# Attention stage reordered, last stage in four steps over blocks, zero fill in parts: one change to a two-layer decoder step on eight cores

## The chip, the cores and the metric

The kernel runs on one Trainium2 chip, as one program on all 8 of its cores, each with its own prompt of 2048 tokens and 16 of the 128 sample tokens. The metric is the device time of the slowest core in microseconds. An engine is TensorE (PE), VectorE (DVE), ScalarE (ACT), GpSimd (POOL) or SyncE (SP); each works through its own instructions in order and waits on semaphores.

## The reference, cut to what matters

```python
def run(x, p, conv_past, kv_past):                      # D = 1024
    h = x
    for i in range(2):
        hn = rms_norm(h, norm_mix[i])
        if i == 0:
            y = conv_module(hn, ...)                    # GLU, depthwise conv, layer norm, product
        else:
            q = project_q(hn, w_q, q_norm)              # 16 heads of 64, each head normed
            y = window_attention(q, k_sh, v_sh, sinks) @ w_o    # window of 128 keys, 4 key heads
        h = h + y
        hn = rms_norm(h, norm_ffn[i])
        h = h + (swiglu(hn) if i == 0 else moe_swiglu(hn))      # D_FF 2816; 8 experts, top 2, 3584 each
        h = h + sigmoid(rms_norm(h, norm_ple[i]) @ w_gate) * (p[i] @ w_proj)
        if i == 0:
            k_sh, v_sh = shared_kv(h)                   # keys normed
    return h, states
```

The outputs are both streams h, the last 30 rows of the convolution's input, and the last 128 keys and values of each sequence.

## The kernel before, in words

The work of a core is cut into blocks of 128 tokens: 16 prompt blocks and block 16 with the 16 sample tokens (NB = 17). The stages follow one another: convolution (to about 230 us), its second product and norms (to 380), the dense SwiGLU's gate and up products (to 727, lines L1353 to L1373, for each of 22 tiles f of the hidden width, over five column groups), its down product with the first per-layer embedding (to about 990), attention (to about 1610), the experts (to about 2858) and the last stage.

A small scheduler (`Sched`) writes waits from declared reads and writes. Every engine and DMA queue runs in the order in which the Python text emits instructions; this order is written by hand. A write has to wait for all earlier readers of its resource; with `part=True` it does not wait for other part writes. A tile `Res` marked `excl` (a PSUM bank) is handed over whole.

*Zeros.* `zerofill` (L325) writes zeros over the 5120 rows of XG, into which tokens are scattered for the experts, and over the 128 dummy rows of YD. Both are issued from ScalarE ahead of the loop over f, from tile `zt` (L1428). Ahead of them SyncE issues three copies of caches to the outputs (ks, vs, convs).

*Attention.* A loop of 21 turns (from L1939) works on several blocks at a time. In turn i block ord5[i] (the sample block is first) is turned for TensorE (`x3_turn`), gives keys and values (`kv_mm`) and queries (`q_mm` twice), is normed by head (`qk_norm` L1682, with the power on GpSimd at L1689), scaled (`qk_scale`) and turned (`qk_turn`, one turn later); block ord5[i-2] has its four groups of scores, exponentials, masks (L1762, L1764) and value products (`pv`, L1783) and is divided (`onorm` L1791 to L1795); the block before is multiplied by w_o (`oproj` L1814, L1819) and its sum normed (`o_norm`: square L944, epsilon on VectorE L948, power on GpSimd L949, scaling L1833); and the one before that is routed (`route_l` L343). `x3_scale` (square, epsilon, power, scaling L1639) prepares block i+1. All but scores and value products use three PSUM banks in rotation (`mb`). For groups of blocks (0 to 4, 5 to 9, 10 to 13, 14 and 15, and 16), `wave_a` and `wave_b` work out expert, rank and slot of each token on VectorE, and GpSimd scatters the normed rows (L161). In the middle of `wave_b` VectorE overwrites the slots that the scatters read (L432), and waits for them. For turns 2 to 5 the 16 sample tokens are attended over their caches at the end of the turn.

*Last stage.* `final_prep` loads the weights of the second embedding into ring slots that are free early, `final` allots the rest. Each block is in three steps: `st0` loads h (SyncE), p (GpSimd's queue), gathers its two expert outputs and turns p by a DMA transpose; `st1` adds the two outputs, weighted by the gates (L786, VectorE, twice), norms (`rstd` L337 to L340), scales (L792) and turns x by a DMA transpose; `st2` has the products (L812, L805), the sigmoid (L819), the gating product (L820) and the sum with h on GpSimd (L822). The second gather of a pair waits for the first one's landing (`part=(k == 1)`).

The central lines of the last stage's loop are these.

```python
for i in range(NB + 1):
    if i < NB:
        b[i] = st1(*a.pop(i))
    if i >= 1:
        st2(*b.pop(i - 1))
    if i + 3 < NB:
        a[i + 3] = st0(i + 3)
```

## Time and profile before

| | us |
|---|---|
| median of 3 runs | 3117.32 (3114.04 to 3370.99) |
| the profiled execution | 3120.35 |
| its span on the slowest core (3) | 3119.0 |
| spans of the eight cores | 3095.4 to 3119.0 |
| TensorE busy | 2466.9 (79%) |
| VectorE, ScalarE, GpSimd busy | 964.4, 743.6, 594.3 |

The profile is of one execution, on the slowest core. Times in it run from the span's start. An arrow `<-` in brackets names what ended the idle time before an instruction; SPq, ACTq and POOLq are the DMA issues of an engine. "x8" is a count of instructions. PEclk is the TensorE clock that was granted, as a share of 2.4 GHz: at any time it is one of 1.2 and 2.4 GHz, and a stretch shows the mean.

### The profile page before, as it was taken

How to read it: one execution, taken by the hardware profiler on the slowest of the kernel's cores; microseconds unless marked ns; L12 is line 12 of the kernel's file. 1: busy time of each engine (PE TensorE's matmuls, PEld its weight loads, DVE VectorE, ACT ScalarE, POOL GpSimd, SP SyncE). 2: the span in 40 equal slices, each digit the busy share in tenths (PEclk: the TensorE clock that was granted, in tenths of full speed). 3: DMA queues.
4: the chain of work that ended last, by engine and by line, in shares of the span. 5: the costliest groups of instructions: out<-in, count | busy, mean ns of one | idle time of the engine just before them, and what ended most of it. 6: DMA issues, size and time to landing. Idle time of an engine off the chain costs nothing.

```text
span 3119.0 us, 43753 instructions; the slowest of 8 cores (3095.4 to 3119.0 us)
## 1 busy us (share of the span) xinstructions
PE 2466.9 (79%) x18903; PEld 1687.7 (54%) x18911; DVE 964.4 (31%) x1492; ACT 743.6 (24%) x1074; POOL 594.3 (19%) x794
## 2 busy tenths in 40 slices
PE   5876749997998266656519999999999999996354
PEld 3453425553443033323218888887799888885111
DVE  4665502221333144444422121211122212120444
ACT  4215401111221354434302111111122111110111
POOL 1105400000000142232331111111121111110444
PEclk8988879998999578778759999999999999998677
DMA  7555584323222510110159999998899999962453
GB/s 194 105 110 139 144 205 72 58 38 65 72 72 72 170 48 30 41 64 31 58 122 177 170 183 167 184 168 154 136 171 181 173 178 177 175 103 66 127 145 94
DMA packets 156458, 377.44 MB, mean 121 GB/s; under 512 B 52424, under 2 KB 61768, under 8 KB 155264
## 3 DMA queue, kind: packets, MB, share of 16 engines
q0 software_dynamic: 69360, 230.65, 43.9%
q1 hardware_dynamic: 81616, 133.15, 14.7%
q10 hardware_dynamic: 5280, 10.75, 1.0%
q8 instruction: 151, 2.47, 0.3%
q14 instruction: 51, 0.42, 0.0%
HBM read 510.55 MB, written 74.24 MB: 187 GB/s over the span
## 4 chain that ended last, share of the span: by engine, by line
PE 63%; issue 11%; POOL 8%; DVE 6%; ACT 4%; DMA 4%; ACTq 2%; SPq 1%; DVEq 0%; POOLq 0%
PE pb L549 25%; PE pb L577 13%; PE pb L1366 9%; PE pb L1479 5%; PE pb L1101 4%; ACTq L149 2%; POOL arena L1689 2%; POOL arena L822 2%; PE pb L1677 1%; PE pb L930 1%; ACT arena L944 1%; POOL arena L161 1%; PE pb L1312 1%; ACT arena L939 1%; DMA arena<-x 1%
## 5 line engine op out<-in xcount | busy, mean ns | idle before, releaser
L549 PE MATMUL pb<-arena 128*128 128x0 bf16 x7168 | 792.4, 274 | 0.8 <-DVE arena L510 0.8
L549 PEld LDWEIGHTS pb<-arena 128*128 128x128 bf16 x7168 | 675.1, 98 | 114.8 <-issue 1.0
L577 PE MATMUL pb<-arena 128*128 128x0 bf16 x3584 | 404.1, 274 | 0.0
L557 DVE TENSOR_TENSOR arena<-arena,pb 128x640 bf16<-128x640 f32 x224 | 183.9, 821 | 650.8 <-PE pb L549 650.8
L577 PEld LDWEIGHTS pb<-arena 128*128 128x128 bf16 x3584 | 336.2, 98 | 55.6
L1366 PE MATMUL pb<-arena 128*128 128x413 bf16 (+1 forms) x1760 | 312.2, 340 | 43.2 <-ACT arena L1372 43.2
L930 PE MATMUL pb<-arena 128*128 128x128 bf16 (+1 forms) x1180 | 106.6, 248 | 269.4 <-DVE arena L1833 111.8
L556 ACT ACTIVATE arena<-pb 128x640 f32<-128x640 f32 x224 | 157.9, 705 | 618.5 <-PE pb L549 618.5
L1366 PEld LDWEIGHTS pb<-arena 128*128 128x128 bf16 x1760 | 172.7, 98 | 181.5 <-ACT arena L1372 43.6
L930 PEld LDWEIGHTS pb<-arena 128*128 128x128 bf16 (+1 forms) x1180 | 83.1, 113 | 299.5 <-DVE arena L1833 114.7
L149 POOL DMA_DIRECT2D arena<-moe_gu x224 | 118.3, 542 | 588.1 <-PE pb L549 253.4
L805 PE MATMUL pb<-arena 128*128 128x512 bf16 (+1 forms) x272 | 93.8, 521 | 129.4 <-DMA arena<-arena 129.4
L944 ACT ACTIVATE arena<-arena 128x1024 bf16<-128x1024 f32 (+1 forms) x85 | 89.8, 1056 | 348.4 <-DVE arena L1484 183.5
L1479 PE MATMUL pb<-arena 128*128 128x512 bf16 (+1 forms) x748 | 166.2, 382 | 0.7 <-DVE arena L1373 0.7
L1373 DVE TENSOR_TENSOR arena<-arena,pb 128x413 bf16<-128x413 f32 (+1 forms) x110 | 64.2, 585 | 289.6 <-PE pb L1366 234.2
L149 POOL DMA_DIRECT2D arena<-moe_d x128 | 67.6, 528 | 385.8 <-PE pb L549 378.1
L939 ACT COPY arena<-pb 128x1024 bf16<-128x1024 bf16 (+6 forms) x142 | 112.3, 793 | 100.3 <-PE pb L1677 45.4
L805 PEld LDWEIGHTS pb<-arena 128*128 128x128 bf16 (+1 forms) x272 | 33.0, 127 | 190.7 <-DMA arena<-arena 138.2
L1101 PE MATMUL pb<-arena 128*128 128x413 bf16 (+1 forms) x640 | 125.2, 360 | 7.0 <-ACT arena L939 7.0
L1372 ACT ACTIVATE arena<-pb 128x413 f32<-128x413 f32 (+1 forms) x110 | 56.6, 516 | 296.0 <-PE pb L1366 240.2
L1479 PEld LDWEIGHTS pb<-arena 128*128 128x128 bf16 (+1 forms) x748 | 72.6, 98 | 87.2 <-issue 2.6
L949 POOL TENSOR_TENSOR arena<-arena 128x1 f32<-128x1 f32 (+1 forms) x68 | 37.5, 552 | 349.3 <-DVE arena L948 349.3
(201 smaller groups left out, 2342.7 us busy)
## 6 DMA issues: line engine op xcount, KB each, us to landing
arena<-moe_gu POOLq DMA_DIRECT2D x224, 512.0 KB, 35.2
arena<-moe_d POOLq DMA_DIRECT2D x128, 448.0 KB, 33.3
arena<-x SPq DMA_DIRECT2D x32, 512.0 KB, 7.7
arena<-ffn_gu POOLq DMA_DIRECT2D x22, 512.0 KB, 5.2
XG<-arena ACTq DMA_DIRECT2D x1, 10240.0 KB, 65.8
arena<-XG SPq DMA_DIRECT2D x8, 1280.0 KB, 39.5
YD<-arena SPq DMA_DIRECT2D x8, 1280.0 KB, 21.8
h1D<-arena SPq DMA_DIRECT2D x16, 512.0 KB, 3.9
```

What stands on the lines that cost most here:

```text
L149: inst = self.E[q].dma_start(out=out, in_=in_)
L549: last = e.matmul(bank(b + h, HALF).shape_from_register(sr), w[:, a, kc, :], xg[:, kc, h * HALF:(h + 1) * HALF].shape_from_register(sr), s ...
L556: S.op("act", lambda e: e.activation(out=sg, in_=self.two(bG), func=AF.Silu), r=[b_r[bG], b_r[bG + 1]], w=[sg_r])
L557: S.op("dve", lambda e: e.tensor_tensor(out=self.hx[:, f, :].rearrange("p (h c) -> p h c", h=2), in0=sg, in1=self.two(bU), op=ALU.mult), r ...
L577: last = e.matmul(bank(b + h, HALF).shape_from_register(sr), w[:, k, :], self.hx[:, f, h * HALF:(h + 1) * HALF].shape_from_register(sr), s ...
L805: last = e.matmul(bank(bG + h2, 512, n), xT[:, kc, 0:n], self.Wg[kc // 2][:, kc % 2, h2 * 512:(h2 + 1) * 512], start=(kc == 0), stop=(kc = ...
L930: last = e.transpose(out=bankb(bk)[:, k * 128:k * 128 + n], in_=src[0:n, (k0 + k) * 128:(k0 + k + 1) * 128], identity=identb[0:n, 0:n])
L939: S.op("act", lambda e: e.copy(out=dst, in_=src), r=r, w=w, part=part)
L944: S.op("act", lambda e: e.activation(out=junk, in_=src, func=AF.Square, scale=1.0 / 32.0, accum_out=ms), r=r, w=[w, jr])
L1101: last = e.matmul(bank(bk_, n), W[:, a, kc, :], xnT[:, kc, s0:s0 + n], start=(kc == 0), stop=(kc == 7))
L1366: last = e.matmul(bank(bk_, n), W[:, a, kc, :], xnT2[:, kc, s0:s0 + n], start=(kc == 0), stop=(kc == 7))
L1479: last = e.matmul(bank(bk + h_, 512, n), lt, Wd[:, f, h_ * 512:(h_ + 1) * 512], start=(f == 0), stop=(f == NF - 1))
```

## The change

The change does three things.

1. The zero fill of XG is cut into four parts, issued from SyncE behind the products of tiles f = 3, 7, 11 and 15; the zeros of YD go with the first. The scatters wait for a resource of their own, `zf_r`. The three copies of caches move behind tiles 5, 9 and 13.
2. The attention loop is put in another order. The epsilon adds of the two block norms go to GpSimd (`powp`); each norm is parted into its square (`x3_sq`, `o_sq`) and its scaling, with other work between; queries and keys are in two buffers (`qkb`) and scaled in the next turn (`qk_scale`, with the two key products as `kk_gain` behind the first squares); the norm and routing of the sample block go through the same path one turn later; the next block is loaded at the end of a turn. The exponential of a wave moves from `wave_a` to `wave_b`.
3. The last stage becomes four steps over blocks: residual and norm of block i, scaling and turning of block i-1, products and output of block i-3. The turns are done by TensorE and ScalarE instead of DMA transposes; one of the two weighted expert outputs is scaled on ScalarE and added on VectorE; the final sum moves from GpSimd to VectorE; gathers don't wait for each other; six buffers for h, four of them in the space of the experts' inputs.

```diff
-    def zerofill(self, z, z_r, nz):
+    def zerofill(self, z, z_r, k, of, behind):
...
-        S.dma("act", xr, z.unsqueeze(1).to_broadcast([128, na, nz]), "zf0", r=[z_r], w=[self.XG_r])
-        S.dma("act", self.YD[NEXP * CAP:NEXP * CAP + 128, :], z[:, 0:D], "zf1", r=[z_r], w=[self.YD_r], part=True)
+        n = NEXP * CAP // of
+        xr = self.XG[k * n:(k + 1) * n, :].rearrange("(a p) d -> p a d", p=128)
+        S.dma("sp", xr, z.unsqueeze(1).to_broadcast([128, n // 128, D]), "zf%d" % k, r=[z_r, behind], w=[self.zf_r], part=True)
+        if k == 0:
+            S.dma("sp", self.YD[NEXP * CAP:NEXP * CAP + 128, :], z, "zfy", r=[z_r], w=[self.YD_r], part=True)
...
-    tl.zerofill(zt, zt_r, D)
...
+        if f in (3, 7, 11, 15):
+            tl.zerofill(zt, zt_r, f // 4, 4, hact_r(f))
+        if f in copies:
+
+            S.dma("sp", copies[f][0], copies[f][1], "d2d%d" % (f // 4 - 1), r=[hact_r(f)])
...
+    def powp(ms, rs, ms_r, rs_r, n):
+
+        S.op("pool", lambda e: e.tensor_scalar(out=ms, in0=ms, scalar1=EPS, scalar2=None, op0=ALU.add), w=[ms_r])
+        S.op("pool", lambda e: e.tensor_tensor(out=rs, in0=ms, in1=nhalf[0:n, 0:1], op=ALU.pow), r=[ms_r, c_eps], w=[rs_r])
```

The attention loop after the change, without the sample block's parts:

```python
        if s_ is not None:
            scores(s_, 0)
        xt = x3_turn(*xs_) if xs_ is not None else None
        xs_ = None
        qt = qk_scale(*qn) if qn is not None else None
        qn = None
        if s_ is not None:
            scores(s_, 1)
        rs_ = [o_sq(n_) for n_ in (rn, r16) if n_ is not None]
        rn = r16 = None
        if qt is not None:
            kk_gain(*qt)
        if xt is not None:
            vb = kv_mm(*xt)
        rs_ = [o_scale(*v) for v in rs_]
        if s_ is not None:
            pv(s_, 0)
            scores(s_, 2)
        ot = o_turn(*on) if on is not None else None
        on = None
        xq = x3_sq(ord5[i + 1]) if i + 1 < 17 else None
        if xt is not None:
            q_mm(*xt, 0, *vb[2:4])
        if s_ is not None:
            pv(s_, 1)
            scores(s_, 3)
        lts = [x_turn(*v) for v in rs_]
        if xq is not None:
            xs_ = x3_scale(*xq)
        if xt is not None:
            q_mm(*xt, 1, *vb[2:4])
            qn = qk_norm(xt[0], xt[1], *vb)
        if qt is not None:
            qk_turn(*qt[0:7])
        if s_ is not None:
            pv(s_, 2)
        if ot is not None:
            oproj(*ot, 0)
        if s_ is not None:
            pv(s_, 3)
            on = onorm(s_)
        if ot is not None:
            oproj(*ot, 1)
            rn = ot[0]
        if pend_wave is not None:
            tl.wave_b(*pend_wave, mb(), 0, xns)
            pend_wave = None
        for lt in lts:
            b = mb()
            tl.route_l(*lt, b, 0)
            done_l.append(lt[0])
```

The last stage's loop after the change, and its steps:

```python
        def resid(n_):
            ...
            S.op("act", lambda e: e.activation(out=t[0:n, :], in_=yy[0:n, 1, :], func=AF.Copy, scale=self.gates[0:n, n_, 1:2]), r=[yy_r, self.g_r[n_]], w=[t_r])
            S.op("dve", lambda e: e.scalar_tensor_tensor(out=h[0:n, :], in0=yy[0:n, 0, :], scalar=self.gates[0:n, n_, 0:1], in1=h[0:n, :],
                                                         op0=ALU.mult, op1=ALU.add), r=[yy_r, self.g_r[n_]], w=[h_r])
            S.op("dve", lambda e: e.tensor_tensor(out=h[0:n, :], in0=h[0:n, :], in1=t[0:n, :], op=ALU.add), r=[t_r], w=[h_r])
...
        for i in range(NB + 3):
            a, b, c = i < NB, 1 <= i < NB + 1, i >= 3
            if b:
                scale(i - 1)
            if a:
                resid(i)
                norm(i)
            if c:
                bP = proj(i - 3)
                sg, sg_r = gate(i - 3)
            if b:
                x_turn(i - 1)
            if 1 <= i < NB - 1:
                p_turn(i + 1)
            if c:
                out(i - 3, bP, sg, sg_r)
            if i + 3 < NB:
                gather(i + 3)
                load(i + 3)
```

Here `norm` is the square on ScalarE and two small GpSimd instructions, `scale` one VectorE product, `x_turn` and `p_turn` are TensorE transposes copied out by ScalarE, `proj` and `gate` the products and the sigmoid, and `out` VectorE's gating product, VectorE's sum and the store.

## Rows read from the trace of the kernel before

**Rows 1.** The page, granted TensorE clock in 40 slices (tenths).
```profile
PEclk8988879998999578778759999999999999998677
```
**Rows 2.** Windows: busy PE, PEld, DVE, ACT, POOL; PEclk, DMA share, GB/s.
```profile
1872.00:1950.00 78.00, 78.00 (x734) 68.27 (x734) 11.49 (x16) 12.07 (x17) 11.60 (x22) 1.00 1.04 167
78.00:156.00 78.00, 68.41 (x439) 37.58 (x438) 47.52 (x53) 16.95 (x26) 7.85 (x14) 0.91 0.56 105
1411.00:1438.00 27.00, 17.49 (x132) 8.92 (x132) 12.20 (x26) 13.11 (x17) 7.24 (x6) 0.81 0.11 40
2858.00:3119.00 261.00, 109.57 (x340) 39.55 (x340) 115.77 (x86) 37.98 (x52) 108.72 (x84) 0.71 0.48 129
```
**Rows 3.** Waits from 370 to 460 us: total, times, longest.
```profile
ACT arena L1372 <- issue: 55.5, 1, 55.5
...
PE pb L1366 <- ACT arena L1372: 43.2, 1, 43.2
```
**Rows 4.** Waits: 1384 to 1438.5 us, then 1327 to 1372 us.
```profile
ACT arena L1639 <- POOL arena L949: 18.1, 3, 6.0
...
DVE arena L432 <- DMA XG<-arena: 14.3, 1, 14.3
```
**Rows 5.** Line L1689, its instructions of the whole span.
```profile
L1689 POOL TENSOR_TENSOR arena<-arena x17: 3532/3910/3912, 1077.5 to 1520.1; 128x20 f32<-128x20 f32 x16, 16x20 f32<-16x20 f32 x1
```
**Rows 6.** Timeline of GpSimd, starts of L1689: start, duration, instruction.
```profile
1202.56 3.91 POOL L1689 TENSOR_TENSOR arena<-arena 128x20 f32<-128x20 f32 x1 [13.25 <-DVE arena L1688]
...
1271.62 3.91 POOL L1689 TENSOR_TENSOR arena<-arena 128x20 f32<-128x20 f32 x1 [14.39 <-DVE arena L1688]
...
1327.02 3.91 POOL L1689 TENSOR_TENSOR arena<-arena 128x20 f32<-128x20 f32 x1 [12.07 <-DVE arena L1688]
...
1371.09 3.91 POOL L1689 TENSOR_TENSOR arena<-arena 128x20 f32<-128x20 f32 x1 [13.69 <-DVE arena L1688]
...
1480.70 3.91 POOL L1689 TENSOR_TENSOR arena<-arena 128x20 f32<-128x20 f32 x1 [12.07 <-DVE arena L1688]
```
**Rows 7.** Timeline of the last stage.
```profile
2876.99 2.60 DVE L786 SCALAR_TENSOR_TENSOR arena<-arena 128x1024 f32<-128x1024 bf16 x2 [18.79 <-DMA arena<-YD,arena]
...
2960.19 4.56 DVE L786 SCALAR_TENSOR_TENSOR arena<-arena 128x1024 f32<-128x1024 bf16 x2
2960.35 3.32 POOL L822 TENSOR_TENSOR arena<-arena 128x1024 f32<-128x1024 f32 x1 [2.58 <-DVE arena L820]
...
2969.98 0.94 POOL L161 DMA_INDIRECT arena<-YD,arena  x1 [4.35 <-DMA arena<-YD,arena]
...
2973.95 4.56 DVE L786 SCALAR_TENSOR_TENSOR arena<-arena 128x1024 f32<-128x1024 bf16 x2
```
**Rows 8.** DMA issues from 370 to 760 us: KB each, median us to landing.
```profile
arena<-ffn_gu POOLq DMA_DIRECT2D x17, 512.0 KB, 5.2
```
**Rows 9.** The chain of waits of the whole span: start, us, what.
```profile
439.42 287.57 PE pb L1366 x1632
...
1609.59 23.73 issue
```
**Rows 10.** Timeline of TensorE around 1395 us.
```profile
1394.97 1.90 PE L1814 MATMUL pb<-arena 128*128 128x512 bf16 x8
1396.71 0.40 PE L1783 MATMUL pb<-arena 128*128 128x65 bf16 x8
```
**Rows 11.** Groups by line and form from 2870 us: busy us, mean ns.
```profile
L792 DVE SCALAR_TENSOR_TENSOR arena<-arena 128x1024 bf16<-128x1024 f32 x16 | 20.6, 1284 | 85.1 <-POOL arena L340 85.1
L820 DVE TENSOR_TENSOR arena<-arena,pb 128x1024 f32<-128x1024 f32 x16 | 19.4, 1214 | 5.0 <-ACT arena L819 5.0
...
L337 ACT ACTIVATE arena<-arena 128x1024 bf16<-128x1024 f32 x16 | 16.9, 1057 | 165.3 <-DVE arena L786 165.3
L819 ACT ACTIVATE arena<-pb 128x1024 f32<-128x1024 f32 x16 | 16.3, 1021 | 35.2 <-PE pb L805 35.2
```
**Rows 12.** The same view from 752 to 990 us, one group.
```profile
L1526 DVE TENSOR_TENSOR arena<-arena 128x1024 f32<-128x1024 f32 x14 | 17.1, 1224 | 0.5
```

More of the change, by code:

```diff
@@ L748, in fbuf, with halves @@
         return self.A.new(o, shape, dt)
+    def halves(self, k, shape):
+        out = []
+        for i in range(k):
+            if i % 2 == 0:
+                o = self.free[self.fslot]
+                self.fslot += 1
+            out.append(self.A.new(o + 2048 * (i % 2), shape, BF16))
+        return Ring(out)
     def final(self):
-        S, A, T, bank, b_r = self.S, self.A, self.T, self.bank, self.b_r
-        pc0, pc0_r = A.new(self.free[self.fslot], [128, 32])
-        self.fslot += 1
@@ L777, in st0, with gather @@
+        def gather(n_):
+            n = rows(n_)
             yy, yy_r = yr.next()
@@ new lines, in turns, with fn, p_turn @@
+        def turns(src, src_r, b, nk, n):
+            def fn(e):
+                last = None
+                for k in range(nk):
+                    last = e.transpose(out=bank(b).bitcast(BF16)[:, k * 128:k * 128 + n], in_=src[0:n, k * 128:(k + 1) * 128], identity=self.idb[0:n, 0:n])
+                return last
+            S.op("pe", fn, r=[src_r, self.id_r], w=[b_r[b]])
+        def p_turn(n_):
+            n = rows(n_)
+            p, p_r = ps.pop(n_)
+            b = self.nb(1)
+            turns(p, p_r, b, 2, n)
+            pT, pT_r = self.pt.next()
+            S.op("act", lambda e: e.copy(out=pT[:, :, 0:n], in_=turned(b, 2, n)), r=[b_r[b]], w=[pT_r])
+            pts[n_] = pT, pT_r
@@ new lines, in x_turn, with proj, fp @@
+        def x_turn(n_):
+            n = rows(n_)
+            x_, x_r = xs.pop(n_)
+            b = self.nb(1)
+            turns(x_, x_r, b, 8, n)
+            xT, xT_r = xt.next()
+            S.op("act", lambda e: e.copy(out=xT[:, :, 0:n], in_=turned(b, 8, n)), r=[b_r[b]], w=[xT_r])
+            xts[n_] = xT, xT_r
+        def proj(n_):
+            n = rows(n_)
+            pT, pT_r = pts.pop(n_)
+            b = self.nb(2)
+            def fp(e):
+                last = None
+                for h2 in range(2):
+                    for kc in range(2):
+                        last = e.matmul(bank(b + h2, 512, n), pT[:, kc, 0:n], self.Wp[:, kc, h2 * 512:(h2 + 1) * 512], start=(kc == 0), stop=(kc == 1))
+                return last
+            S.op("pe", fp, r=[pT_r, self.Wp_r], w=[b_r[b], b_r[b + 1]])
+            return b
@@ L801, in fg, with gate @@
+        def gate(n_):
+            n = rows(n_)
+            xT, xT_r = xts.pop(n_)
+            b = self.nb(2)
             def fg(e):
@@ L804, in fg @@
                     for kc in range(8):
[L805 removed]
+                        last = e.matmul(bank(b + h2, 512, n), xT[:, kc, 0:n], self.Wg[kc // 2][:, kc % 2, h2 * 512:(h2 + 1) * 512], start=(kc == 0), stop=(kc == 7))
                 return last
[L808 to L813 removed]
@@ new lines, in final @@
+        for k in range(3):
+            load(k)
+        for k in range(3):
+            gather(k)
+        for k in range(2):
+            p_turn(k)
+        for i in range(NB + 3):
[14 more added lines that the diff above has]
+                out(i - 3, bP, sg, sg_r)
@@ L1653, in kv_mm @@
         b = mb()
+        qkf, qkf_r = qkb.next()
         def fk(e):
@@ L1668, in kv_mm, with q_mm @@
             copy("act", vb[:, :, 0:64], V.rearrange("p (g d) -> p g d", g=4), [b_r[b]], [vb_r])
-        return vb, vb_r
-    def q_mm(n_, n, xT, xT_r, h):
+        return vb, vb_r, qkf, qkf_r
+    def q_mm(n_, n, xT, xT_r, h, qkf, qkf_r):
         b = mb()
```

263 lines of the change are left out of this document (121 added, 142 removed).

## The prediction

> **What bounds the kernel now.** I read the granted TensorE clock by slice of the page first [rows 1]: it is 9 (90% or more) in the expert stage, 8 or 9 in most of what comes before, and low in three places: 7 in the slice from 390 us, 5 to 8 in the attention stage (1014 to 1638 us), 6 and 7 in the last stage (from 2886 us). The expert stage (1638 to about 2858 us) is TensorE from end to end (the stretch 1872 to 1950: busy 78.00 of 78 us, clock 1.00) [rows 2], and the change edits nothing in it. So its worth is decided in the three places, and each is read by what is late there.
>
> First place: the waits of 370 to 460 us [rows 3]. ScalarE issues the 10 MB of zeros, and its next issue (the zeros of YD) holds it for 55.5 us; TensorE's products for w_gate/w_up find no free bank and stand 43.2 us.
>
> Second place: attention, 17 blocks and a drain. The windows, from 1411 to 1438 us, say [rows 2] that a usual turn of 27 us holds 17.5 us of TensorE at a clock of 0.81, 13.1 of ScalarE, 12.2 of VectorE and 7.2 of GpSimd: nothing is full, so the turn is a chain of waits. Its largest link is ScalarE at the scaling of the next block (L1639), which waits 18.1 us in three turns for the small power on GpSimd [rows 4]: VectorE's epsilon add and GpSimd's two key products stand before that power. I measure turns by the starts of L1689, one in each turn [rows 5, 6]: 17 starts, 1077.5 to 1520.1 us, 442.6 us for 16 intervals. They are 125.1 us for the first six, 69.1 for two around the sample block, 55.4 for two plain ones, 44.1 for one with five blocks scattered to the experts (wave_b), 109.6 for four plain ones (27.4 each) and 39.4 for one with the second wave.
>
> Third place: the last stage, 261 us from 2858 to 3119 [rows 2]. One block takes 13.8 us, from 2960.19 to 2973.95 [rows 7]. The order on VectorE is scale, product, two sums; then ScalarE's square, the power, and on GpSimd that power stands behind the 3.32 us sum of L822 and the second gather, which waits for the first one's landing. The two product-sums took 4.56 us beside L822 and 2.60 us without it [rows 7]. Then the DMA transpose and only then the gate products.
>
> **The change part by part.**
>
> *Zeros in parts on SyncE, copies behind products.* ScalarE issues none of them. What it removes is the 43.2 us stall, and TensorE's return to full clock after it, about 1.5 us (my estimate: a few products at half clock). What it adds: five DMA issues and three moved copies on SyncE, which has nothing to do there until the stage after; SyncE may now stand behind a full queue without anybody waiting. The same bytes now lie beside weight loads, which took 5.2 us to land [rows 8] and are issued five tiles ahead; a tile f of five column groups costs 14 us of TensorE (287.57 us for 1632 of its matmuls, 80 to a tile) [rows 9], so a landing may grow tenfold before a product waits. Bounds: 30 us (weights late at some tile) to 46 us. I take 45.
>
> *Attention, reordered.* Work per turn stays, but the epsilon adds of two norms go to GpSimd (2 x 0.2 us, inside its idle time), qkf gets a second buffer (query scaling can lie in the next turn), a square and its scaling are parted by a product, and the next block's load is issued at the end of the turn (h is needed one half-turn later; SyncE has h4D's store ahead of it, done early in the turn). I laid one turn out in the new order, each engine in order, three PSUM banks in rotation, ScalarE about 14 us in all. TensorE's demand at full clock: an 8-matmul product of 512 columns lets its follower start 1.74 us later [rows 10], and a group of scores about 0.32 (an estimate: four matmuls of 256 columns, of which some run side by side); five products, four scores, four value products (0.3 each), four turns (together 2.0) and routing (0.2) make 13.4 us, 15.7 if every group's whole duration is summed. In the layout the first value product starts at 4.5 us, q's second product ends at 11.2, qk_turn's bank is free at 10.8, the first output product waits for ScalarE's copy until 12.6, the second starts at 14.9 and routing ends at 17.1. So 17.2 us with TensorE never at half clock. It would be busy some 85%, and the row that is nearest in that (78 to 156 us: 68.4 of 78 us busy) has clock 0.91 [rows 2]. That adds a little over a microsecond: 18.5 us a turn. Lower bound 16.5 (the demand above plus the waits for a bank); upper bound 24, if one link of the old chain remains.
>
> Plain turns: six of (55.4 + 109.6) / 6 = 27.5, less 18.5, make 54. The wave turns: VectorE waits 14.3 us for scatters to land before it may overwrite the slots [rows 4]; that edge stays, and TensorE can run some 5 us ahead of it, so 18.5 + 10.5 = 29 each, against 83.5 for both: 25. Two around the sample block: 69.1 against 2 x 26 (its own products and its wave of two scatters): 17. First six: 125.1 against 102 (two light turns of 10, four of 20.5 with the sample's keys, whose serial transposes, exponentials and values stay at the end of a turn): 23. Drain, 1520.1 to 1609.6 us [rows 5, 9], 89.5 us: three turns without a new block save 3 each: 9. The first expert's load, the 23.73 us gap after that [rows 9], is untouched. Sum 128 us; with turns of 24 it is about 55, with 16.5 about 155.
>
> *Last stage as four steps.* VectorE gets one block's scaling, product-sum, sum, gating product and final sum, in turn for three different blocks: 1.28 + 1.28 + 1.22 + 1.21 + 1.22 [rows 7, 11], the added f32 sums by L1526 [rows 12]. That is 6.2 us, but in-order queues close a longer loop: the sum of block i, its square on ScalarE (1.06 [rows 11], with its accumulator read 1.25), the sigmoid of block i-3 behind it (1.02), then VectorE's product and final sum. So 1.28 + 1.28 + 1.22 + 1.25 + 1.02 + 1.21 + 1.22 = 8.5, with five handovers 8.8. TensorE: 20 products and ten small transposes, some 5 us at full clock, 9.5 at half. The gate product waits until the product of the block before has left its two banks, about 1.2 us before the turn begins, and must end 5 us into it; at half clock throughout it ends at 5.7. I take 9.0. GpSimd holds two gathers that no longer wait for each other, a load and the small norm ops, 4 us; the sum on GpSimd is gone, and so is the slowing of the VectorE sums beside it. ScalarE: 1.05 + 1.25 + 1.02 + two copies 1.4 = 4.7.
> Then: first sum at about 2872 instead of 2877 (gathers back to back, h loaded into buffers that are free early); three turns without gates, 17 us; 14 full ones, 126; three without a new block, 21; landing 3: end at 3039, 80 us saved. With 8.5 it is 87, with 11 (transfers or half clock) 52.
>
> **Sum.** Of the profiled execution (3120.35 us, span 3119.0): 3120.35 - 45 - 128 - 80 = 2867. It stands 3 us above the median of the runs (3117.32), so I forecast 2865 to 2870, and write 2869.
>
> **A rule that speaks against it.** The rows show 1.00 in the densest stage with all eight cores at work [rows 2]. The Trainium skill (TensorE: Matmul & The Clock Gate, section What's actually happening, with its warnings under Seeing it yourself) says that a current limiter takes a die to 13/16 of the clock once three of its cores run dense products. By that rule the fuller attention turns would run at 0.81 even when never idle; the trace does not bear it out in the expert stage, which is denser.
>
> **Rivals.**
> (A) Attention keeps one link. Three banks turn under eleven uses a turn; if a copy on ScalarE or the power behind the key products is late, the turn is near 24 us and the end is 2869 + 73 = 2942. For: ScalarE has 14 us of the 18.5 and its order interleaves seven producers. Against: its longest wait today is for one power [rows 4], which is moved ahead of the key products. Chance 0.15.
> (B) The last stage is held by transfers or by the half clock: each block moves 1.7 MB, 190 GB/s at 9 us, where the stage now moves 129 [rows 2]. 11 us a block: 2897. Chance 0.13.
> (C) Both stages better: attention 16.5, last stage 8.5: 2869 - 27 - 7 = 2835. Chance 0.15.
> (D) The dense turns are granted less than 1.00: 13.4 us at the 0.81 that the present turn has [rows 2] is 16.5, with 3.8 us of waits 20.3 a turn, 1.8 x 16 = 29 more: 2898. For: nothing in a row. The page named above would have it so. Chance 0.04.
> (E) The zeros do not do what they say: parts or copies in front of weight loads stall products as long as before, 45 back: 2914. Chance 0.04.
> (F) Slower than before. The new order closes a cycle through the three banks so that a turn is serial: TensorE 17.5, ScalarE 13.1 and VectorE 12.2 end to end are 42.8 us, 24.3 above my turn over 16 turns: 389 more, 3258. It decides from a turn of 34 us (251 / 16 = 15.7 above 18.5). Against: most copies have two group lengths of other work beside them. Chance 0.02.
> My own case: 0.47, 2869, by itself 2845 to 2900. All cases: 2825 to 2950. A measurement tells 2% from no change; 2% is 62 us. Faster 0.96, same 0.02, slower 0.02.
>
> **What would show it.** Zeros: no wait of TensorE over 5 us between 380 and 720 us; a tile stays at 14 us. Attention: the starts of the head power (L1689 today) 18 to 19 us apart, about 29 at two waves, clock 0.9; VectorE's wait for scatters still near 14 us. ScalarE's scaling no longer waits 6 us for the power. Last stage: 9 us a block, 3.3 us sums gone from GpSimd, no DMA transposes, VectorE's sum 1.2. Expert stage: same length within 3 us. Wrong if turns stay above 22 us or products wait for weights in the first place.

## The result, and the profile after

The kernel after takes 2869.70 us (median of 4 runs, 2863.77 to 3135.99), the kernel before 3126.84 us on the same chip; the ratio is 0.919, with a 95% interval of 0.914 to 0.923. (Ratios leave out executions in which a die was slowed; the upper ends of some ranges below come from these, and where a die of an experiment's profile was, the other die's cores are read.) Each ratio, here and below, is to the kernel before on the same chip. The forecast was 2869 us. The total is right to a microsecond, and as the terms below show, that is luck: misses of both signs cancel.

The profiled execution after has spans of 2844.8 to 2868.7 us by core. To see where the time went I cut each core's span at five places that both kernels have (the end of the products for w_gate/w_up, the first and the last start of the small head power on GpSimd, the first product of the experts, their last) and took the mean over the eight cores. An ordinary table, worked out from the first and last times of these lines:

```
us, mean of 8 cores              before   after   difference   forecast
to the last w_gate/w_up product   719.7   697.0      -22.7        -45
from there to the 1st head power  346.6   347.6       +1.0          0
16 turns of attention             444.1   329.8     -114.3       -119
drain and start of the experts    115.8    89.1      -26.7         -9
experts                          1220.0  1219.3       -0.7          0
last stage                        261.1   173.3      -87.8        -80
```

Each column is one execution. Three kernels of the experiments below have the old last stage unchanged (p_zero, p_attn, p_rows), and it takes 256 to 257 us in them, so the last row's gain is 83 to 88 us. The first row's times lie within some 4 us of these in other executions that share the code.

The page of the kernel after, for [rows 1]: granted TensorE clock in 40 slices.

```profile
PEclk8896899999999867989779999999999999999878
```

The eight slices from 359 to 932 us (a slice is 71.7 us) are all 9 now; attention, from the 15th to the 20th, has 6, 7, 9, 8, 9, 7, and the last three are 8, 7, 8. Windows of the kernel after, core 4, for [rows 2] (us, busy PE, PEld, DVE, ACT, POOL, then PEclk, DMA share, GB/s): an unchanged stretch ahead of the zeros, four plain turns of attention, experts, last stage.

```profile
78.00:156.00 78.00, 68.41 (x430) 37.16 (x429) 46.83 (x51) 18.62 (x29) 7.36 (x13) 0.91 0.55 105
1278.00:1345.00 67.00, 56.16 (x529) 30.99 (x527) 50.95 (x102) 52.22 (x69) 35.11 (x28) 1.00 0.15 56
1700.00:1778.00 78.00, 78.00 (x683) 63.81 (x682) 11.91 (x16) 10.81 (x15) 11.07 (x21) 1.00 1.04 167
2740.00:2840.00 100.00, 74.77 (x356) 32.53 (x354) 70.39 (x59) 51.85 (x72) 39.62 (x54) 0.81 0.55 166
```

Core 4 is the slowest, and its last stage is not like the others': in the same window the other seven cores were granted 0.91 to 0.93. This is core 0:

```profile
2740.00:2840.00 100.00, 71.00 (x368) 31.90 (x373) 69.24 (x58) 47.75 (x67) 35.70 (x46) 0.93 0.52 152
```

The four plain turns were granted 1.00 on all eight cores, each read at its own time.

First place: the waits from 365 to 705 us, for [rows 3] (total, times, longest).

```profile
DVE arena L1453 <- DMA XG<-arena: 51.7, 4, 13.7
...
PE pb L1446 <- DVE arena L1453: 16.0, 7, 3.5
DVE arena L1453 <- DMA ks<-ck: 14.8, 1, 14.8
DVE arena L1453 <- DMA vs<-cv: 14.7, 1, 14.7
DVE arena L1453 <- DMA convs<-sc: 13.8, 1, 13.8
```

The 55.5 us of ScalarE and the 43.2 of TensorE are gone. In their place stand seven waits of VectorE (95.0 us together), one for each of the four zero transfers and three copies, and TensorE stands behind them seven times, 16.0 us. The weights, for [rows 8]: they took 6.5 us to land instead of 5.2, and no wait of TensorE is for them; a part of the zeros takes 12.7.

```profile
XG<-arena SPq DMA_DIRECT2D x4, 2560.0 KB, 12.7
arena<-ffn_gu POOLq DMA_DIRECT2D x17, 512.0 KB, 6.5
```

Second place: the starts of the head power (L1689 before, L1779 after), for [rows 5, 6]; the columns are start, duration, instruction, idle time before it.

```profile
1240.78 3.54 POOL L1779 TENSOR_TENSOR arena<-arena 128x20 f32<-128x20 f32 x1 [5.86 <-DVE arena L1778]
...
1277.83 3.54 POOL L1779 TENSOR_TENSOR arena<-arena 128x20 f32<-128x20 f32 x1 [7.32 <-DVE arena L1778]
...
1294.50 3.54 POOL L1779 TENSOR_TENSOR arena<-arena 128x20 f32<-128x20 f32 x1 [5.56 <-DVE arena L1778]
...
1311.17 3.54 POOL L1779 TENSOR_TENSOR arena<-arena 128x20 f32<-128x20 f32 x1 [5.56 <-DVE arena L1778]
```

A plain turn is 16.67 us (1294.50 to 1311.17), the turn with the first wave 37.05 (1240.78 to 1277.83). What is late in that one (waits from 1240 to 1278 us, for [rows 4]): VectorE's wait for the scatters, and behind it ScalarE and TensorE as long.

```profile
ACT arena L1856 <- PE pb L1850: 18.6, 2, 15.9
...
PE pb L1877 <- DVE arena L1858: 15.6, 1, 15.6
DVE arena L432 <- DMA XG<-arena: 14.6, 1, 14.6
```

The start of the experts, for the 23.73 us gap of [rows 9]; in the kernel before, GpSimd began its 27 weight loads ahead of SyncE's load of the gathered rows. First the kernel before, then the one after, timelines of core 3.

```profile
1604.67 14.37 POOL L149 DMA_DIRECT2D arena<-moe_gu  x27
1606.93 0.37 SPq L149 DMA_DIRECT2D arena<-XG  x1
```

```profile
1447.23 13.12 SPq L149 DMA_DIRECT2D arena<-XG  x2
1447.74 14.36 POOL L149 DMA_DIRECT2D arena<-moe_gu  x27 [2.31 <-DMA XG<-arena]
1455.43 3.12 PEld L502 LDWEIGHTS pb<-arena 128*128 128x128 bf16 x30 [18.40 <-issue]
```

After, the order is turned round: GpSimd waits 2.31 us for the scatters, and the rows go first. The addresses in the kernel say why. The first ring slot begins at byte 102208 of a partition and is 4096 long; the first buffer of the normed rows, from which the last block is scattered, begins at 104320 with the second query buffer ahead of it and began at 99200 without. The traces part the 26.7 us of this row. From the last head power to the issue of the rows it is 86.5 us before and 75.1 after (the drain, 11.3 less); from there to TensorE's first instruction on them (L502) it is 24.1 us before and 9.0 after (15.2 less), in the mean of the cores.

Last stage, timeline of core 4, for [rows 7]:

```profile
2738.30 1.28 DVE L803 SCALAR_TENSOR_TENSOR arena<-arena 128x1024 f32<-128x1024 bf16 x1
2739.68 1.23 DVE L805 TENSOR_TENSOR arena<-arena 128x1024 f32<-128x1024 f32 x1
2740.94 1.06 ACT L812 ACTIVATE arena<-arena 128x1024 bf16<-128x1024 f32 x1 [4.04 <-DVE arena L805]
...
2743.48 1.22 DVE L886 TENSOR_TENSOR arena<-arena,pb 128x1024 f32<-128x1024 f32 x1 [2.57 <-ACT arena L881]
...
2744.73 1.22 DVE L889 TENSOR_TENSOR arena<-arena 128x1024 f32<-128x1024 f32 x1
...
2745.88 1.28 DVE L821 SCALAR_TENSOR_TENSOR arena<-arena 128x1024 bf16<-128x1024 f32 x1
...
2747.07 1.28 DVE L803 SCALAR_TENSOR_TENSOR arena<-arena 128x1024 f32<-128x1024 bf16 x1
```

The block's sum (L805) ends, ScalarE's square starts after 4.04 us of idling, VectorE's product waits 2.57 us for the sigmoid behind that square, and the next block's scaling follows the final sum. That is the ring of the prediction, turn after turn: starts of L803 on this core are 8.77, 8.33, 8.75 and 8.33 us apart, 8.54 in the mean of twelve. On the other seven cores, at the higher clock, they are 8.32 to 8.36 apart. In the turn shown the sigmoid (L881) waits 0.33 us more for TensorE's gate product, which took 4.72 us; in the next turn it follows the square at once. So the slowest core pays 0.2 us a block for the clock.

### The profile page after: what moved, and what is told of

The parts are those of the page before. It is cut to its first block and busy times, and to the rows that moved or that the text cites. A ratio compares the mean times of both kernels' runs of the same rounds, so it can differ in the third digit from the quotient of the medians.

```text
span 2868.7 us, 44068 instructions; the slowest of 8 cores (2844.8 to 2868.7 us)
## 1 busy us (share of the span) xinstructions
PE 2447.2 (85%) x19073; PEld 1691.0 (59%) x19081; DVE 952.5 (33%) x1458; ACT 777.8 (27%) x1125; POOL 570.3 (20%) x828
## 5 line engine op out<-in xcount | busy, mean ns | idle before, releaser
L549 PEld LDWEIGHTS pb<-arena 128*128 128x128 bf16 x7168 | 676.7, 98 | 116.8 <-issue 1.1
L577 PEld LDWEIGHTS pb<-arena 128*128 128x128 bf16 x3584 | 336.4, 98 | 56.0
L1446 PEld LDWEIGHTS pb<-arena 128*128 128x128 bf16 x1760 | 171.7, 98 | 154.9 <-DVE arena L1453 18.8
L1010 PE MATMUL pb<-arena 128*128 128x128 bf16 (+1 forms) x1180 | 100.0, 239 | 181.6 <-ACT arena L1728 62.3
L1010 PEld LDWEIGHTS pb<-arena 128*128 128x128 bf16 (+1 forms) x1180 | 79.0, 108 | 218.2 <-ACT arena L1728 63.3
L1560 PE MATMUL pb<-arena 128*128 128x512 bf16 (+1 forms) x748 | 166.8, 383 | 0.7 <-DVE arena L1453 0.7
L1453 DVE TENSOR_TENSOR arena<-arena,pb 128x413 bf16<-128x413 f32 (+1 forms) x110 | 63.1, 584 | 263.1 <-PE pb L1446 164.7
L1560 PEld LDWEIGHTS pb<-arena 128*128 128x128 bf16 (+1 forms) x748 | 72.7, 98 | 87.7 <-issue 3.5
L877 PE MATMUL pb<-arena 128*128 128x512 bf16 (+1 forms) x272 | 82.2, 471 | 31.7 <-DVE arena L886 31.7
L1181 PEld LDWEIGHTS pb<-arena 128*128 128x128 bf16 x640 | 65.8, 104 | 65.0 <-issue 16.3
L583 ACT CAST arena<-pb 128x640 bf16<-128x640 f32 x32 | 22.1, 692 | 299.5 <-PE pb L577 299.5
## 6 DMA issues: line engine op xcount, KB each, us to landing
XG<-arena SPq DMA_DIRECT2D x4, 2560.0 KB, 12.7
```

The source lines that it names most:

```text
L549: last = e.matmul(bank(b + h, HALF).shape_from_register(sr), w[:, a, kc, :], xg[:, kc, h * HALF:(h + 1) * HALF].shape_from_register(sr), s ...
L577: last = e.matmul(bank(b + h, HALF).shape_from_register(sr), w[:, k, :], self.hx[:, f, h * HALF:(h + 1) * HALF].shape_from_register(sr), s ...
L877: last = e.matmul(bank(b + h2, 512, n), xT[:, kc, 0:n], self.Wg[kc // 2][:, kc % 2, h2 * 512:(h2 + 1) * 512], start=(kc == 0), stop=(kc == 7))
L1010: last = e.transpose(out=bankb(bk)[:, k * 128:k * 128 + n], in_=src[0:n, (k0 + k) * 128:(k0 + k + 1) * 128], identity=identb[0:n, 0:n])
L1181: last = e.matmul(bank(bk_, n), W[:, a, kc, :], xnT[:, kc, s0:s0 + n], start=(kc == 0), stop=(kc == 7))
L1446: last = e.matmul(bank(bk_, n), W[:, a, kc, :], xnT2[:, kc, s0:s0 + n], start=(kc == 0), stop=(kc == 7))
```

## The experiments

**The three parts alone.** Each part of the change was put by itself into the kernel before. In words:

```diff
 p_zero: before, with zerofill in four parts, zf_r and the moved copies
 p_attn: before, with the reordered attention loop, x3_sq, o_sq, powp, qkb
 p_final: before, with the last stage in four steps and its buffers
```

> The kernel before with only the zeros and the copies of the changed one. My theory: ScalarE's 43 us stall goes, and the copies behind the products are entered as readers of the hidden activations, so VectorE waits 12 to 15 us for each to land and TensorE about 16 us in seven places; 23 to 27 us are gained, 3092 to 3096 by the median before of 3117. Rival, the prediction's own: 45 us are gained, 3072. Rival: the parts only cost TensorE as long as before, 3117.

Measured: 3090.38 us, ratio 0.992 (0.988 to 0.995) to 3121.89. This is less than the 2% that the forecast calls a change, but its interval leaves out 1, and the first stage ends at 694 us in the mean of the cores (719.7 before). VectorE waits for the zeros here too, 56.8 us in four waits, and 11.2 us for a copy; TensorE waits behind it six times, 13.0 us.

> The kernel before with only the attention stage of the changed one (with its shifted layout). Theory: the terms add up, 113 us in the 16 intervals and 28 in the drain and the first expert's start, 141 us gained, about 2976. Rival, the prediction's sum: 128 us, about 2989. Rival: part of the gain rests on the other two parts, 3000 or above.

Measured: 2970.57 us, ratio 0.952 (0.949 to 0.955). 16 turns take 328.2 to 330.8 us by core, and from the last head power to the first expert product it is 87.9 to 89.6. The total is that of the first theory (2976), though in the profiled execution cores 0 and 1 ended the first stage at 743 and 739 us, the other six at 712 to 722.

> The kernel before with only the last stage of the changed one. Theory: it gives its whole 88 us alone, 3029. The prediction's term was 80, 3037. The stage is 173 us from the last expert product to the end, 8.5 us a block.

Measured: 3025.68 us, ratio 0.971 (0.967 to 0.975); the last stage takes 174.4 us (mean of the cores), its other stages are within 3 us those of the kernel before.

What follows: no sign that the parts touch each other. 1 less each ratio gives 0.8, 4.8 and 2.9%, together 8.5%; all three at once gave 8.1%, within the intervals. The zeros alone bring about 25 us, not 45, and the attention part alone brings the whole gain at the start of the experts.

**The order of rows and weights.** Is the shorter start of the experts the drain's doing, or that the rows are now loaded ahead of the weights? One line in the kernel before makes GpSimd wait for the scatters before its weight loads:

```diff
     tl.ring_open(0, tl.RING_N)
+    S.deps("pool", [tl.XG_r], [])
```

> The kernel before with one wait: GpSimd starts the expert weights only when the last scatter has landed, as SyncE's load of the first expert's rows does. Theory: the rows' load then shares the queues with fewer weights ahead of it and lands 10 to 15 us sooner than the 25 us that it takes now; 10 to 17 us gained, about 3103. Rival: the order of the two makes nothing, and the shorter start of the changed kernel comes from the attention's drain; 3117 or a little above, as weights start 3 us later.

Measured: 3100.90 us, ratio 0.993 (0.991 to 0.995). From the last head power to the first expert product: 101.4 us against 115.8. The other stages, which the edit leaves alone, are up to 4 us shorter too in this execution (the last stage 257.0 against 261.1), so the reading rests on the stage and not on the total, whose ratio is again within 2% of 1. The DMA issues of core 3 from 1575 to 1640 us, kernel before and then this one (KB each, median us to landing):

```profile
arena<-moe_gu POOLq DMA_DIRECT2D x27, 512.0 KB, 53.0
arena<-XG SPq DMA_DIRECT2D x2, 1280.0 KB, 25.2
```

```profile
arena<-moe_gu POOLq DMA_DIRECT2D x28, 512.0 KB, 46.1
arena<-XG SPq DMA_DIRECT2D x2, 1280.0 KB, 15.8
```

The rows were issued 1.9 us behind the start of the weights before and 0.4 us ahead of it here (means of the cores). So 14 us of the 27, by this run, are this order, and what is left agrees with the 11.3 us that the traces give to the drain.

**Readers.** In the kernel after each zero or copy transfer waits behind a tile's products by being entered as a reader of `hact_r(f)`, though it moves nothing of that buffer. One such resource stands for 15 tiles, so its next writer is VectorE's next product (L1453), which then waits until the transfer has landed. Here SyncE waits for the same thing but is not entered as a reader:

```diff
-        S.dma("sp", xr, ..., "zf%d" % k, r=[z_r, behind], w=[self.zf_r], part=True)
+        S.deps("sp", [behind], [])
+        S.dma("sp", xr, ..., "zf%d" % k, r=[z_r], w=[self.zf_r], part=True)
...
-            S.dma("sp", copies[f][0], copies[f][1], "d2d%d" % (f // 4 - 1), r=[hact_r(f)])
+            S.deps("sp", [hact_r(f)], [])
+            S.dma("sp", copies[f][0], copies[f][1], "d2d%d" % (f // 4 - 1))
```

> The changed kernel, but SyncE waits for a tile's products before it issues zeros and copies without being entered as a reader of the hidden activations. Theory: VectorE's seven waits of 12 to 15 us for these transfers go, and with them TensorE's 16 us; 16 to 18 us gained, 2853, and the prediction's 45 us for this part is then right but for that edge. Rival: the transfers slow the weight loads and TensorE waits for these instead; 2870.

Measured: 2845.58 us, ratio 0.913 (0.909 to 0.917). The first stage ends at 675.6 us (mean), 21.4 earlier than in the kernel after and 44.1 earlier than in the one before: the forecast's 45, with some 4 us between executions of the same code. The largest wait of VectorE from 365 to 705 us is now for TensorE's products, and none is for zeros or copies (one of 11.2 us, for a block's load, belongs to the next stage):

```profile
DVE arena L1454 <- PE pb L1447: 241.4, 109, 2.8
```

**The row numbers of a wave.** The scatters read a tile that VectorE writes again at once, and it waits 14.6 us for their landing. A resource of its own for the copied row numbers lets VectorE go on:

```diff
-        dv(lambda e: e.tensor_copy(out=pairs(slg), in_=sx), w=[g_r])
+        sl_r = Res()
+        dv(lambda e: e.tensor_copy(out=pairs(slg), in_=sx), r=[g_r], w=[sl_r])
...
-                       ..., r=[xn_r, g_r, self.zf_r], w=[self.XG_r], part=True)
+                       ..., r=[xn_r, sl_r, self.zf_r], w=[self.XG_r], part=True)
```

> The changed kernel, with a resource of its own for the slots that the scatters read, so that VectorE does not wait for their landing in wave_b. Theory: two turns of 36 to 37 us lose most of VectorE's 14.6 us waits, GpSimd's 12.5 us of scatter issues still hold the small powers of the next turn back some 6 us; 10 us gained at each, 5 more in the drain, 2845. Rival: GpSimd's queue is the real bound of these turns and nothing is gained; 2870.

Measured: 2852.35 and 2847.94 us, ratio 0.915 (0.911 to 0.919). The total can't be told from the kernel after (0.914 to 0.923); the stage can. On cores 0 to 3 the 16 turns take 315.4 us (329.8 in the kernel after), and the two wave turns 31.7 each instead of 37.05 and 35.6. The timeline of core 2:

```profile
1228.28 3.54 POOL L1780 TENSOR_TENSOR arena<-arena 128x20 f32<-128x20 f32 x1 [5.87 <-DVE arena L1779]
1260.00 3.54 POOL L1780 TENSOR_TENSOR arena<-arena 128x20 f32<-128x20 f32 x1 [7.10 <-DVE arena L1779]
```

The wait for the scatters was worth 9.2 us of the two wave turns, and 4.9 more in the turn with the sample block's wave (20.5 instead of 25.4 us). A wave turn still costs 15 us more than a plain one. In it GpSimd issues ten scatters from 1235.45 to 1248.31 us, and the small norm instructions of the next blocks follow directly; no run takes them away, so what each part of the wave costs is not shown.

**The final sum on GpSimd.** One piece of the last stage undone:

```diff
-            S.op("dve", lambda e: e.tensor_tensor(out=o[0:n, :], in0=sg[0:n, :], in1=h[0:n, :], op=ALU.add), r=[sg_r, h_r], w=[o_r])
+            S.op("pool", lambda e: e.tensor_tensor(out=o[0:n, :], in0=sg[0:n, :], in1=h[0:n, :], op=ALU.add), r=[sg_r, h_r], w=[o_r])
```

> The changed kernel with the last stage's final sum back on GpSimd, all else as it is. Theory: the sum leaves the loop (1.2 us a block less) but runs 3.3 us beside VectorE's sums of two SBUF operands, which then lose some 2 us, and GpSimd's power waits behind it; 0.8 us a block more, 11 to 15 us slower, about 2883. Rival: the loop is what counts and it gets shorter, 2853. The prediction put no figure on it alone.

Measured: 2881.64 us, ratio 0.924 (0.918 to 0.929); the last stage takes 187.3 us instead of 173.3, as the first theory had it. Timeline of core 4:

```profile
2770.93 3.33 POOL L889 TENSOR_TENSOR arena<-arena 128x1024 f32<-128x1024 f32 x1 [1.03 <-DVE arena L886]
2771.97 3.38 DVE L803 SCALAR_TENSOR_TENSOR arena<-arena 128x1024 f32<-128x1024 bf16 x1
```

The product-sum L803 takes 1.28 us alone and 3.38 beside the sum: GpSimd's ends at 2774.26, VectorE's 1.09 later. Taking the sum's 1.22 us off VectorE has put 2.10 on. The Trainium skill (SBUF — State Buffer, section Who interferes with whom) says that a VectorE instruction with two inputs in SBUF and a GpSimd instruction that reads SBUF exclude each other for the whole instruction; by that rule VectorE's would end its own 1.28 us after GpSimd's, and the trace, with 1.09, agrees to 0.2 us.

**Two orders for the last stage's ring.** First an order in which outputs come ahead of the scaling and of the second sum:

```diff
+            if a:
+                resid(i)      # product-sum only; the second sum moves into norm
             if c:
                 bP = proj(i - 3)
                 sg, sg_r = gate(i - 3)
+                out(i - 3, bP, sg, sg_r)
             if b:
+                scale(i - 1)
                 x_turn(i - 1)
+            if a:
+                norm(i)
```

> The changed kernel with another order in the last stage: sigmoid, gating product and output of block i-3 before the second sum and the square of block i, scaling of block i-1 between. Theory: the 8.5 us of a block are the loop of sum, square, sigmoid, product and final sum; without the square in it VectorE's 6.2 us or TensorE's gate, sigmoid, product (3.6 + 1.0 + 1.2) bound it; 6.8 us a block, 24 us gained, 2846. Rival: transfers or half clock bound the block and it stays at 8.5; 2870.

Measured: 2921.50 us, ratio 0.938 (0.934 to 0.942): 52 us longer, where 24 less were expected. The waits from 2740 to 2840 us, core 4:

```profile
DVE arena L888 <- ACT arena L883: 47.5, 8, 6.5
...
PE pb L834 <- DVE arena L823: 43.4, 9, 4.8
```

TensorE's turning of a block (L834) now stands behind the scaling, which stands behind the output, which waits for the sigmoid of a product that stands behind the last turning: one ring over three engines. Starts of L803 are 11.4 and 12.5 us apart by turns, 11.9 a block. The clock was 0.77 to 0.79 on all cores in this window, so how much of the 11.9 is the ring and how much the clock is not parted. I had counted TensorE's gate product, but not the turning ahead of it in TensorE's queue.

So the second order changes one thing, the square behind the sigmoid on ScalarE:

```diff
             if a:
                 resid(i)
-                norm(i)
             if c:
                 bP = proj(i - 3)
                 sg, sg_r = gate(i - 3)
+            if a:
+                norm(i)
```

> One edit of the kernel after: in the last stage the norm of block i (ScalarE's square, then GpSimd's sum and power) is entered behind the sigmoid of block i-3 instead of ahead of it; no work is added or left out. In the kernel after a block takes 8.54 us, while no engine is busy for more than 74.8 of 100 us, and three waits stand in each turn: ScalarE's square for VectorE's residual sum (4.0 us), VectorE's product for the sigmoid (2.6), TensorE's projection for VectorE's product (3.3). Theory (a ring of waits: VectorE's scaling and two residual sums, then the square, then the sigmoid, which stands behind the square on ScalarE, then VectorE's product and sum, then the next turn's scaling): with the sigmoid ahead of the square the ring is cut, since the gate's products don't depend on this turn's residual. A block then takes what the busiest engine does, TensorE's 0.748 x 8.54 = 6.4 us to about 7.0, the last stage is 17 x 1.5 to 17 x 2.1 = 26 to 36 us shorter, and the time 2834 to 2845 us. Rival 1 (the clock and the transfers set the pace: 0.81 of the clock, 166 GB/s): a block stays at 8.3 to 8.6 and the time within 4 us of the kernel after's 2869.7. Rival 2 (what an earlier order of this stage showed, in which TensorE fell to half clock and a block took 11.4 us): the time is over 2885.

Measured: 2848.47 us, ratio 0.912 (0.909 to 0.915); the last stage takes 152.8 us, 20.5 less, where 26 to 36 were expected. Timeline and window, core 4:

```profile
2746.01 1.28 DVE L821 SCALAR_TENSOR_TENSOR arena<-arena 128x1024 bf16<-128x1024 f32 x1 [0.77 <-POOL arena L814]
2747.22 1.28 DVE L803 SCALAR_TENSOR_TENSOR arena<-arena 128x1024 f32<-128x1024 bf16 x1
2748.60 1.23 DVE L805 TENSOR_TENSOR arena<-arena 128x1024 f32<-128x1024 f32 x1
2749.76 1.21 DVE L886 TENSOR_TENSOR arena<-arena,pb 128x1024 f32<-128x1024 f32 x1
2751.00 1.23 DVE L889 TENSOR_TENSOR arena<-arena 128x1024 f32<-128x1024 f32 x1
2751.11 1.20 POOL L813 TENSOR_SCALAR arena<-arena 128x1 f32<-128x1 f32 x1 [0.97 <-ACT arena L812]
...
2753.00 1.28 DVE L821 SCALAR_TENSOR_TENSOR arena<-arena 128x1024 bf16<-128x1024 f32 x1 [0.78 <-POOL arena L814]
```

```profile
2720.00:2820.00 100.00, 71.58 (x421) 34.16 (x426) 85.71 (x72) 61.61 (x85) 66.84 (x63) 1.00 0.64 193
```

The ring was the bound: a block takes 6.99 us (2746.01 to 2753.00), with 193 GB/s moved, so the transfers had not set the pace. The clock rose with it, on this core from 0.81 to 1.00 and on the others from about 0.91 to 0.98 or more; that the clock is not what made the block short is shown by two cores of the last experiment. The block is as expected (6.4 to 7.0 us), but the expectation took the saving 17 times: only the last 13 of the 16 intervals between blocks are shorter, the first three take 6.1 us in both kernels. What holds a block at 7 us is again a ring, over VectorE (busy 85.71 of 100 us) and GpSimd: the small add of the norm (L813) took 0.23 us in the kernel after and takes 1.20 here, beside VectorE's final sum, with which it ends (from its start to the power's 1.29 us against 0.31); the power and VectorE's scaling stand behind it.

**Epsilon adds.** The adds of the attention stage's block norms back on VectorE:

```diff
-        powp(ms, rs, ms_r, rs_r, n)
+        powh(ms, rs, ms_r, rs_r, n)
```

> The kernel after, with the small adds of the block norms in the attention stage put back from GpSimd to VectorE (the power stays on GpSimd). In the plain turns of the kernel after (16.67 us each) VectorE is busy for 50.95 and GpSimd for 35.11 of 67 us, and neither is the busiest. Theory: the turn is set by the chain over TensorE and ScalarE, and some 34 adds of about 0.1 us and their hops change nothing: 2869.7 within 6 us, turns of 16.6 to 16.9 us. Rival: the hop VectorE to GpSimd for the power puts 0.3 to 0.6 us in each of 17 turns, since VectorE takes the add in order behind its large operations: 5 to 10 us more in all, 2875 to 2880. Rival: less work on GpSimd makes the turns shorter, 2860.

Measured: 2878.46 us, ratio 0.921 (0.918 to 0.925). The total can't be told from the kernel after, but the stages can: the 16 turns take 336.7 us (336.0 to 337.9 by core) against 329.8 (328.4 to 331.0), 0.43 us a turn in the mean and in a plain one (17.1 us), and the first rival stands. I had priced the move of these adds at nothing; why it is worth more than their own 0.2 us (perhaps the place in VectorE's queue ahead of the power; the clock of the plain turns fell from 1.00 to 0.98 as well) no run here takes apart.

**All together.** The three edits that gained, in one kernel: transfers not entered as readers, the wave's row numbers, the square behind the sigmoid.

> The kernel after with three edits: the zero and copy transfers wait for the products but are no longer entered as readers (2845.58 alone against 2869.7, 24 less), the row numbers of a wave in a tile of their own so that the scatters hold up nothing on VectorE (about 12 less alone), and the norm behind the sigmoid in the last stage (26 to 36 less by the theory of its own run). Theory: the three places don't touch each other, so the gains add: 2869.7 - 24 - 12 - 31 = 2803, 2790 to 2815. Rival (gains overlap: a core that is early waits elsewhere, or the last edit gives nothing): 2830 to 2840.

Measured: 2811.32 us (2810.32 to 2829.57), ratio 0.901 (0.898 to 0.903): the fastest of all, 58 us below the kernel after's 2869.70 and 8 above the middle of what was expected. Turns 315.7 us, last stage 153.9: both gains are whole. Two cores of eight end their first stage at 698.3 and 703.3 us, where the other six do so at 672.0 to 680.8; these two were granted 0.88 of the clock from 100 to 650 us, the others 0.93 to 0.94, and they are the two with the longest spans. Where they lose it shows in the stretch from 110 to 230 us, core 6 and then core 0:

```profile
110.00:230.00 120.00, 120.00 (x758) 70.82 (x757) 76.12 (x77) 19.46 (x31) 3.54 (x7) 0.81 0.30 67
```

```profile
110.00:230.00 120.00, 104.73 (x835) 67.29 (x833) 89.33 (x93) 19.41 (x31) 3.73 (x7) 0.95 0.49 100
```

Core 6 was granted 0.81 with TensorE never idle, and the clock record of its trace holds this one value from 101 to 238 us, so it is not a mean of 1.2 and 2.4 GHz as elsewhere; core 0 did more products in less busy time. Cores 0 and 1 of p_attn and of a_slots show the same. Why these pairs were held there is open. The last stage has another such pair, cores 4 and 5. Core 4 and then core 0:

```profile
2700.00:2780.00 80.00, 68.97 (x337) 30.94 (x341) 69.86 (x58) 51.33 (x72) 58.17 (x55) 0.81 0.71 210
```

```profile
2700.00:2780.00 80.00, 59.68 (x349) 28.32 (x346) 69.52 (x58) 49.22 (x67) 58.90 (x55) 0.98 0.75 217
```

Both take 7.0 us a block (6.99 and 7.01), so in this order of the last stage the clock costs nothing.

## Why the prediction was right, and where it was not

The number 2869 is itself not what the prediction's sum gives. The sum is 2867, for an execution that stood 3 us above the median; taken to the median it is 2864, and the prediction went up to 2869 without a reason. The measured differences add up to 251 us, the forecast terms to 253. So the closeness is luck twice over, and the terms have to be judged one by one.

*Zeros: -22.7 instead of -45, below its lower bound of 30.* The 43.2 us stall went as said. The step that failed is "SyncE may now stand behind a full queue without anybody waiting": somebody waits. The edit adds a reader to a resource that tiles 0 to 14 share (the others share a second one), and VectorE writes it again with its very next product, so seven landings stand in VectorE's queue. I priced the bytes and the queue of the added DMAs and not the dependence that their argument `behind` makes. Without that entry the term measured 44.1 us (a_nomark). The sign for it in the prediction, no wait over 5 us of TensorE, held (3.5 at most), and so would not have found it; VectorE's waits did.

*Attention, 16 turns: -114 instead of -119.* The layout of a plain turn, 17.2 us with a full clock, was near: 16.67 measured at 1.00. What was mis-sized is the step after it, "the row that is nearest in that (78 to 156 us: 68.4 of 78 us busy) has clock 0.91": 84% busy (56.16 of 67 us) was granted 1.00, so the microsecond added for it was none. Against this gain stand the wave turns: 37 and 36 us, forecast 29. TensorE did not run ahead by 5 us; it waited 15.6 us at L1877, as long as VectorE itself. And without VectorE's wait a wave turn is still 15 us above a plain one (a_slots), where the difference in the kernel before, 44.1 less 27.4, held little beside the 14.3 us of waiting. Around the sample block 41.3 and the two after it 42.7 us against 52 and 37; the first six 105.6 against 102.

*Drain and first experts: -27 instead of -9.* "The first expert's load, the 23.73 us gap after that, is untouched" is the step that failed. Nothing in its code changed, but the buffers did, and with them which of two queues issues first; that alone measured 14 us (p_rows). The drain gave 11 instead of 9.

*Last stage: -88 (or -83, by the other executions of the old stage) instead of -80.* The ring was named rightly, 8.5 us with 8.8 for handovers; measured is 8.33 on seven cores, so the handovers are in the durations already. The 9.0 for the half clock was too much: even on core 4, with 0.81 in the window, it is 8.54. That the ring is the cause is shown by a_sqlate, which cuts it; a_sumpool shows that the final sum on VectorE is part of the gain (14 us). What the scaling on ScalarE, TensorE's transposes and the independent gathers bring, each by itself, no run here parts.

*Rivals.* A (a turn of 24 us) did not come. B's bytes are no bound: 193 GB/s are moved at 6.99 us a block. C came in both its sizes, the plain turn at 16.67 and the block at 8.3 to 8.5, but not in its sum; the waves and the zeros took that back. D is out for attention: the clock was 1.00 in four turns, on all eight cores. The Trainium skill's rule that the prediction names (TensorE: Matmul & The Clock Gate, under Seeing it yourself) would have granted 13/16 there, if these turns count as dense. The last stage's 0.81 on core 4 is no case of it: it was a mean of stretches at 1.2 and at 2.4 GHz. But 13/16 itself is in this record, in the pairs of cores of best2, p_attn and a_slots that were granted 0.81 without a break; there it held pairs of cores, where the page speaks of a whole die, and the kernel after's profile has none. E was the nearest to a true one, half of the 45. F did not come.

## What to carry to other kernels

Of each DMA that is "only placed" behind something, ask whether the way of placing it makes it a reader or a writer, and who writes that buffer next: here that cost some 20 us of 44. A pipeline over blocks is as fast as the ring that its queues close, so write down the ring over all engines, and move the instruction that hangs another block's result behind this block's (one line here, 20 us). Where two engines issue loads at about the same time, put the small one that the next product needs first.

## What the runs showed that was not expected

- A load of 1280 KB issued 2.3 us behind the start of 27 weight loads took 25.2 us to land, issued ahead of them 15.8, and the weights landed no later (53.0 and 46.1 us).
- TensorE's busy share was no guide to its granted clock: in one window of the last stage core 4 had 0.81 with 74.77 of 100 us busy and core 0 had 0.93 with 71.00; without the ring core 4 had 1.00 with 71.58; in attention it was 1.00 with 56.16 of 67. A busy share itself grows when the clock is low, since each product then takes longer.
- Two cores can be granted 0.81 for over 100 us, with TensorE never idle, while the other six of the same execution are not (best2, 110 to 230 us).
- A GpSimd sum and a VectorE product-sum, both from SBUF, ran one behind the other (3.33 and 3.38 us), not side by side. It goes the other way too: a GpSimd add of one column, 0.23 us alone, took 1.20 beside VectorE's sum.
